# Places of matmul operands and the order of splits, taps and evacuations in a two-block layer stack

## The reference, cut to what matters

```python
# block 1
for l in range(2):
    x = x + 0.5 * swiglu(rms_norm(x, ffn1_norm[l]), ffn1_w1[l], ffn1_w2[l])      # 1024 -> 2*2816 -> 1024
    x = x + hybrid_mixer(rms_norm(x, mix_norm[l]), ...)
    x = x + 0.5 * swiglu(rms_norm(x, ffn2_norm[l]), ffn2_w1[l], ffn2_w2[l])
x = rms_norm(x, final_norm)
# its mixer: proj = h @ w_in + b_in, cut into pa, pb, pc, pg
y_a = (rg_lru(conv4(pa[:512])) * gelu(pa[512:])) @ lru_w_out      # recurrent branch
y_b = mla_branch(pb)                                              # 8 heads, low-rank q and kv
y_c = silu(layer_norm(conv31(glu(pc)))) @ conv_w_out + b          # depthwise convolution, 31 taps, 512 channels
merged = sum(sigmoid(pg)[i] * y_i); return merged @ w_out
# block 2
for l in range(2):
    x = x + rms_norm_2(hybrid_mixer_2(rms_norm_2(x)), ...)   # 4 fox, 8 nsa (selected, window, compressed), 4 dilated heads
    x = x + rms_norm_2(conv_ffn(rms_norm_2(x)), ...)         # up, 3 taps, silu(a) * b, down
```

## Time and profile before

| | |
|---|---|
| median of 3 runs | 2071.71 us (2068.88 to 2075.6) |
| profiled execution | 2077.53 us, its span 2075.7 us |
| TensorE busy, matmuls | 1994.5 us, 15240 |
| VectorE / ScalarE / GpSimd busy | 1395.0 / 1159.7 / 142.6 us |
| granted TensorE clock, mean | 0.981 |
| read from HBM | 327.27 MB, 158 GB/s over the span |
| costliest | the three products L657 to L659 with h: 2704 matmuls each, and with hid: 1056 each |

### The profile page before, as it was taken

One profiled execution on the slowest core, in us unless ns is written; L12 is line 12 of the kernel. 1 busy time (PEld: TensorE's weight loads), 2 busy tenths in 40 slices (PEclk: granted clock), 3 DMA queues, 4 the chain that ended last, 5 costly groups with the idle time before them and its releaser, 6 DMA issues.

```text
span 2075.7 us, 39521 instructions
## 1 busy us (share of the span) xinstructions
PE 1994.5 (96%) x15240; PEld 1898.6 (91%) x15240; DVE 1395.0 (67%) x2058; ACT 1159.7 (56%) x1847; POOL 142.6 (7%) x153
## 2 busy tenths in 40 slices
PE   7999989999999999999999999998999999899998
PEld 7999988999999999988999999876899998679997
DVE  5765787666655665788666656775698477638963
ACT  5444676564445444676465435665666458556753
POOL 1063100010000001100010001000200010002000
PEclk9999999999999999999999999999999999899999
DMA  5545433455545545443455544531255544203643
GB/s 210 202 166 191 168 127 132 156 189 199 171 168 199 191 154 192 170 150 109 151 193 192 184 156 168 181 123 41 102 187 181 189 144 169 102 24 140 214 156 115
DMA packets 53533, 329.80 MB, mean 159 GB/s; under 512 B 5936, under 2 KB 6704, under 8 KB 27952
## 3 DMA queue, kind: packets, MB, share of 16 engines
q1 hardware_dynamic: 53424, 328.34, 45.4%
HBM read 327.27 MB, written 1.05 MB: 158 GB/s over the span
## 4 chain that ended last, share of the span: by engine, by line
PE 66%; DVE 10%; issue 8%; ACT 5%; DVEq 4%; DMA 4%; POOLq 3%; POOL 1%; ACTq 0%; SPq 0%
PE bank L657 17%; PE bank L658 17%; PE bank L659 17%; PE bank L704 4%; DVE w_lo L636 3%; DMA raw<-in_w 3%; ACT w_hi L597 2%; PE bank L669 1%; PE bank L671 1%; DVE conv L1371 1%; PE bank L1659 1%; PE bank L1643 1%; PE bank L678 1%; DVEq L1365 1%; PE bank L1660 1%
## 5 line engine op out<-in xcount | busy, mean ns | idle before, releaser
L636 DVE TENSOR_TENSOR w_lo<-raw,w_hi 128x2048 fp32r<-128x2048 f32 (+3 forms) x348 | 673.6, 1939 | 326.5 <-ACT w_hi L597 310.6
L657 PE MATMUL bank<-h_hi,w_hi 128*128 128x256 f32 x2704 | 779.8, 288 | 12.2 <-DVE w_lo L636 4.2
L658 PE MATMUL bank<-h_lo,w_hi 128*128 128x256 f32 x2704 | 768.2, 284 | 0.0
L659 PE MATMUL bank<-h_hi,w_lo 128*128 128x256 f32 x2704 | 768.0, 284 | 0.0
L597 ACT ACTIVATE w_hi<-raw 128x2048 fp32r<-128x2048 f32 (+2 forms) x346 | 560.5, 1623 | 138.8 <-DMA raw<-in_w 117.4
L657 PEld LDWEIGHTS bank<-h_hi,w_hi 128*128 128x128 f32 x2704 | 522.2, 193 | 17.6 <-issue 11.7
L658 PEld LDWEIGHTS bank<-h_lo,w_hi 128*128 128x128 f32 x2704 | 522.1, 193 | 1.3
L659 PEld LDWEIGHTS bank<-h_hi,w_lo 128*128 128x128 f32 x2704 | 522.0, 193 | 0.0
L657 PE MATMUL bank<-hid_hi,w_hi 128*128 128x256 f32 x1056 | 295.4, 280 | 0.0
L658 PE MATMUL bank<-hid_lo,w_hi 128*128 128x256 f32 x1056 | 295.4, 280 | 0.0
L659 PE MATMUL bank<-hid_hi,w_lo 128*128 128x256 f32 x1056 | 295.4, 280 | 0.0
(11 more groups left out here) (337 smaller groups left out, 2937.3 us busy)
## 6 DMA issues: line engine op xcount, KB each, us to landing
raw<-in_w SPq DMA_DIRECT2D x198, 1024.0 KB, 4.8
raw<-in_w SPq DMA_DIRECT2D x96, 704.0 KB, 4.1
raw<-in_w SPq DMA_DIRECT2D x52, 768.0 KB, 4.2
raw<-in_w SPq DMA_DIRECT2D x8, 512.0 KB, 3.8
raw<-in_w SPq DMA_DIRECT2D x4, 576.0 KB, 3.7
x<-in_x SPq DMA_DIRECT2D x1, 1024.0 KB, 5.0
out<-x SPq DMA_DIRECT2D x4, 256.0 KB, 2.4
const<-in_const SPq DMA_DIRECT2D x1, 548.0 KB, 5.4
```

The source lines that it names most:

```text
L636: dve.tensor_tensor(w_lo[:, s % SPLIT_SLOTS, 0:n], raw[:, s % RAW_SLOTS, 0:n], w_hi[:, s % SPLIT_SLOTS, 0:n].bitcast(F32), ALU.subtract).t ...
L657: pe.matmul(out, hi, x_hi, start=start, stop=False, skip_group_check=skip)
L658: pe.matmul(out, hi, x_lo, start=False, stop=False, skip_group_check=skip)
L659: return pe.matmul(out, lo, x_hi, start=False, stop=stop, skip_group_check=skip)
```

## The change

Three things are changed.
1. Two unused tiles, of 64 bytes ahead of `x` and of 96 bytes ahead of `hid_hi`, move all that lies behind them. To stay within SBUF, `w_lat` and `rest` become smaller: `LAT_BLOCKS` is 9 instead of 10, and three blocks of uq 2 instead of two lie in `sq`. By the 32-byte rule x, h_hi and h_lo then start 64 bytes past a multiple of 128, and so do hid, m, win and o2; lat, o1 96 past; xa and conv 32 past. The weight tiles stay.
2. Block 1: pb 0 joins the steps at which VectorE (`mixer1_dve`) splits behind its taps; ScalarE's (`mixer1_act`) split behind pb 0 is dropped, so unit 9 is split with unit 10 behind li 1; the 14 taps at li 1 are 7, a split, 7; uk and uv have 1 tap each; stat_mu and stat_ln move one step later; `first_products` and `by_tiles` can take the first tiles of one unit alone (`alone`: 4 in mixer 1, 6 in the second feed-forward layer), and wait for each unit's weights on its own.
3. Block 2's mixer (`mixer2_act`, `mixer2_dve`): cum 1 moves from step 13 to 15, R 7 from 14 to 17; on ScalarE the exp of a head stands behind the transposition's copy and the W evacuation of its step; cmp 0, ca 1, cmp 1, f 6 and f 7 split nothing ahead of themselves, and units f 6, f 7, O 0 to O 3 are split behind named heads.

```diff
+LAT_BLOCKS = 9
-MU_AFTER, LN_AFTER, GATES_AHEAD = 5, 6, 2
+MU_AFTER, LN_AFTER, GATES_AHEAD = 6, 7, 2
...
-               10: [("f", 6), ("c2", 0)], 11: [("cum", 0)], 12: [("SC", 0), ("f", 7)], 13: [("cum", 1), ("R", 6)],
-               14: [("R", 7), ("TC", 0)], 16: [("J", 0)], 17: [("K", 0)], 18: [("K", 1)], 20: [("J", 1)], 21: [("K", 2)], 23: [("K", 3)],
-               25: [("K", 4)], 27: [("K", 5)]}
+               9: [("ct", 0)], 10: [("f", 6), ("c2", 0)], 11: [("cum", 0)], 12: [("SC", 0), ("f", 7)], 13: [("R", 6)],
+               14: [("TC", 0)], 15: [("cum", 1)], 16: [("J", 0)], 17: [("R", 7), ("K", 0)], 18: [("K", 1)], 20: [("J", 1)],
+               21: [("K", 2)], 23: [("K", 3)], 25: [("K", 4)], 27: [("K", 5)]}
+HIGH_BEHIND = {8: ("f", 6), 9: ("f", 7), 10: ("O", 0), 12: ("O", 2), 14: ("O", 3)}
+LOW_BEHIND = {9: ("f", 6), 10: ("f", 7), 11: ("O", 0), 12: ("O", 2), 16: ("O", 3)}
+SPLIT_BESIDE = [("cmp", 0), ("ca", 1), ("cmp", 1), ("f", 6), ("f", 7)]
...
 for n in range(3, len(HEADS2)):
-    at = EVAC2.index(("S", n))
-    EVAC2[at], EVAC2[at + 1] = EVAC2[at + 1], EVAC2[at]
+    step = EVAC2.index(("S", n))
+    EVAC2.remove(("S", n))
+    EVAC2.insert(step + (1 if n == 3 else 2), ("S", n))
...
+        sbuf("offset_h", [P, 16])
         x = sbuf("x", [P, KT, T])
...
+        sbuf("offset_hid", [P, 24])
...
-                w_lat = sbuf("w_lat", [P, 22 * P], F32, early)
+                w_lat = sbuf("w_lat", [P, (12 + LAT_BLOCKS) * P], F32, early)
...
-            sbuf("rest", [P, 3, 4, T], F32, phase)
+            sbuf("rest", [P, T + (12 + LAT_BLOCKS) * P], F32, phase)
...
-        def by_tiles(pe, work, l, groups, tile_ready, tile_used=None, stat_after=None, stat=None):
+        def by_tiles(pe, work, l, groups, tile_ready, tile_used=None, stat_after=None, stat=None, alone=0):
             outs = [(work.out(g)[:, half * T:half * T + T], s, half) for g, s in groups for half in range(2)]
-            for k in range(KT):
+            order = [(k, outs[2 * n:2 * n + 2]) for n in range(2) for k in range(alone)] + [(k, outs) for k in range(alone, KT)]
+            for k, some in order:
                 pe.wait_ge(*tile_ready(k))
+                if alone and k == 0:
+                    weights_ready(pe, some[0][1])
...
-                    first_products(pe, nm, work, l, m, [((up, j), at + j) for j in range(2)], lambda: norm_pe(pe, work, nm, l, n))
+                    if not w:
+                        weights_ready(pe, at + 1)
+                    first_products(pe, nm, work, l, m, [((up, j), at + j) for j in range(2)], lambda: norm_pe(pe, work, nm, l, n),
+                                   6 if w else 0)
...
-            weights_ready(pe, at1 + 1)
             by_tiles(pe, work, l, [(("pa", i), at1 + i) for i in range(2)], lambda k: n1.h_ready(l, KT + k + 1), n1.raw_used,
-                     3, lambda: norm_pe(pe, work, n1, l, 1))
+                     4, lambda: norm_pe(pe, work, n1, l, 1), 4)
...
-                    if i == 0:
-                        split.until(at1 + UNIT_OF[g] + AHEAD)
...
-        TAPS_AT = {("pb", 0): 6, ("pb", 1): 2, "li": 14, "pc": 4, "uq": 2, "uk": 3, "uv": 3, "S": 2, "A": 4, "B": 5}
+        TAPS_AT = {("pb", 0): 6, ("pb", 1): 2, "li": 14, "pc": 4, "uq": 2, "uk": 1, "uv": 1, "S": 2, "A": 4, "B": 5}
...
-                if g in UNIT_OF and kind not in ("A", "B", "lr", "li") and g not in LAST_OUTPUTS and g not in LAST_GATES and g != ("pc", 1):
+                if g in UNIT_OF and kind not in ("A", "B", "lr", "li") and g not in LAST_OUTPUTS and g not in LAST_GATES and g not in TAKEN_FIRST:
                     split.until(at1 + UNIT_OF[g] + AHEAD)
...
-                    convolve(TAPS_AT["li"])
+                    convolve(TAPS_AT["li"] // 2)
                     split.until(at1 + UNIT_OF[g] + AHEAD)
+                    convolve(TAPS_AT["li"] // 2)
...
                     convolve(TAPS_AT[g])
+                    if i == 0:
+                        split.until(at1 + UNIT_OF[g] + AHEAD)
...
-                if g in UNIT_OF2 and kind != "O" and g != ("vb", 1):
+                if g in UNIT_OF2 and kind != "O" and g != ("vb", 1) and g not in SPLIT_BESIDE:
                     split.until(at2 + UNIT_OF2[g] + AHEAD)
...
-                    split.until(freed_by_scores(at2, i))
+                    if i < 8:
+                        split.until(freed_by_scores(at2, i))
                     softmax_act_exp(act, probs2, row2, i % PROBS2, max2_ready(l, i + 1), exp2_ready)
                     for n in due(i, len(HEADS2)):
                         softmax_act_norm(act, probs2, row2, n % PROBS2, sums2_ready(l, n + 1), probs2_ready)
+                    if i in HIGH_BEHIND:
+                        split.until(at2 + UNIT_OF2[HIGH_BEHIND[i]])
...
-                    if i == 14:
-                        split.until(at2 + UNIT_OF2["O", 3])
+                    if i in LOW_BEHIND:
+                        split.until(at2 + UNIT_OF2[LOW_BEHIND[i]])
```

25 lines of the change are left out of this document (13 added, 12 removed), and 2 rows, old and new, of the table MIX2_BESIDE.

## The result

The changed kernel takes 2046.82 us (median of 4 runs, 2041.83 to 2047.12), the kernel before 2073.65 beside it: ratio 0.9866, interval [0.9844, 0.9889]. That is 1.3% faster, 27 us between the medians and 28 us by the ratio. The forecast was 1985 us, 4.2%. The sign is right, the size is not, and the time lies 1 us above the range. The profiled execution has a span of 2045.1 us.

The account below looks back on a forecast made before the run. TensorE's pace, set by operand place, was taken to bound the feed-forward phases. 49.4 (places) + 14.0 (mixer 1) + 23.0 (block 2's mixer) = 86.4 us off 2077.5 gives 1991.1, by the runs' median 1985; range 1936 to 2046.

Parts of the forecast that it names:

- The bound: Feed-forward phases: TensorE, busy 96%, sets the pace, 120.0 ns per matmul with h moving and 117.3 with hid, by operand place.
- Part 1: Operand places, all phases: moved tiles shorten matmul intervals; 31.0 up phases, 8.4 down phases, 10 mixers, sum 49.4 us.
- a straight line through the two places the trace has: Matmul interval by bytes past 128: 120.0 ns at 0, 117.3 at 32, so 114.7 at 64; chance 0.42, 1985 us.
- the mixers' half: Mixers: shorter matmul intervals would give 19.6 us, but another engine decides half of the time, so 10 us.
- The deep rival: All matmuls with moved operands: the extra goes entirely at 64, interval 109.5 ns, 1943 us; chance 0.28.
- The rival of 64 bytes: Operand places: only the place within 64 bytes counts, h stays at 120, hid returns to 120, 2045 us; together 0.15.
- The slower rival: Operand places: 64 is worse than 0, slower overall from an interval of 122.6 ns, 2099 us at 125; chance 0.05.
- The down phases' cap: Down phases: a raw slot's turn of 7.58 us limits each pair of units, so at most 0.24 x 48 = 11.5 us.
- Part 2: Mixer 1 and entry of the second feed-forward layer: reordered splits and taps remove TensorE waits, 2 x (1.7 + 3.3 + 2.0) = 14.0 us.
- What is late next: Mixer 1: unit 9's subtraction 0.7 us late and stat_lat behind pb 2's evacuation; of 3.5 us, 1.7 remain.
- Part 3: Block 2's mixer: two long waits and half the low clock about them go, 6.1 + 5.4 per layer, 23.0 us.
- the waits only move: Reordered mixers: each removed wait is replaced by the next link, only operand places gain, 2022 us; chance 0.10.

Follow-up runs that it names:

- Places alone: The kernel before plus the two offset tiles and the smaller spare tiles making room, no order moved: ratio 0.9933 to before, 14 us.
- the best distance with the early positions: Against the changed kernel: h, hid, m at 112 modulo 256 from weights, win, o2 at 192, position loads at start, R 7, cum 1 back: 1999.8 us.
- weights at 64: The changed kernel with the 64-byte tile ahead of w_hi instead of x, so weights, h and hid all stand at 64: ratio 0.9946 to before.
- the kernel at 192: The changed kernel with all moving operands of three-term products 192 past a multiple of 256 bytes from the weights: 2022.9 us, ratio 0.9747 to before.

## Why the forecast was wrong, point by point

- **The bound** (TensorE's pace, by operand place): right. Places alone gave 14 us with no step moved, and the best distance with the early positions gave 47 us more on nearly the same orders (only R 7 and cum 1 differ).
- **Part 1, the size.** Failed at "I take a straight line through the two places the trace has ... so 114.7 at 64". Two points were joined by a line along an axis, bytes past 128, that is not the chip's: what counts is the distance to the weights modulo 256, and it jumps (64 for hi and lo alike has 117.8 or 113.3, never 114.7). It had to be taken in full address: h stood at distance 0 of 256, hid at 160, and the change brought both to 64. At 117.8 the sum's own terms become 5856 x 2.2 = 13 us, and -3168 x 0.5 = -1.6 in the down phases, where I had +8.4. With the mixers' half, 4 us, that is 15; 14 was measured alone. A unit takes 5.65 and 3.89 us, where 5.5 and 3.79 stood forecast. This term carries 34 of the 58 us by which the sum was too large (86.4 against 28). A second fault is hidden in it: of the 31.0 us for up phases, 34 x 48 x 5.3 = 8.7 were block 2's, and block 2's up phases gave 0.1 us. Block 1's four gave 8.7. That 15 and 14 agree is therefore partly luck.
- **The deep rival** (109.5 ns, 1943 us, chance 0.28): its mechanism exists, its place and size do not: the least is 113.3. **The rival of 64 bytes** (2045 us, chance 0.15) came near the time, for the wrong reason: h did not stay at 120. **The slower rival** (64 worse than 0, from 122.6 ns) had the wrong place but a real mechanism: 123.3 ns at 4 bytes.
- **The half in the mixers.** In block 2's it seems too much: with places alone its two stretches, mixer and up phase, took 2.6 and 1.2 us longer than before, where (504 + 1056) x 2.2 ns = 3.4 us less each would follow from the intervals. The mixers had 61 us at half clock there, against 51 before. This is one execution, the slowest of its five, and not more than a hint, since the same program's mixers differ by 6 us from one execution to the next.
- **The down phases' cap.** The 7.58 us turn of a raw slot was no limit: at 113.3 ns a pair takes 66 x 113.3 = 7.48 us, and such phases take 59.84 us with no wait. Of that turn 1.85 us was waiting for a transfer; since the transfer is issued when the slot comes free, the turn can follow the pace. The forecast's "at most 0.24 x 48 pairs" does not come out of its own numbers either: from 7.74 to 7.58 are 0.16 us, 7.7 us in all, less than the 8.4 it took.
- **Part 2** (14 us): right in kind. T 0's wait (3.3), pb 1's (1.6) and the entry's (2.0) are gone. "What is late next" was named, pb 2's subtraction (0.9) and stat_lat, and the latter was costed too low: it is 2.5 us in layer 0 and 3.9 in layer 1, for q's evacuation behind two copies on ScalarE, where 1.8 us in all were taken off for both. 10 us were measured.
- **Part 3** (23 us): the step that failed is counting each long wait, and half of the low clock about it, as time gained. The waits of the earlier trace rows did go, and about the first the clock rose to 1.00. But all waits of the mixer together fell by only some 2 us in each layer (16.6 to 14.2, 16.1 to 14.4), and at the heads half clock grew from 3 to 10 us, so that block 2's mixers had 44 us of it in after against 51 before (34 to 48 in the other traces of this order). 5 us were measured. The rival "the waits only move" was the right one for this part; it should have been weighed for each part by itself, not for the whole.
- **Range and chances.** The ends were made of single cases; no case held a small gain in part 1 together with a moved part 3, and that is what came: 14 + 10 + 5 = 29 us, each measured by itself.

The Trainium skill's "TensorE: Matmul & The Clock Gate" (section "Back-to-back issue gap") gives N/2.4 + 2.5 ns, 109.2 for 256 columns, as the gap of an isolated matmul, and says itself that with a weight load for each matmul both set the spacing; the forecast left that out. No stretch reached 109.2; the runs show 113.3 to 123.3 by the places of the operands.

Open: why a distance has its interval, why some have two, and how the four tiles of a product act together. That the reads of the weights and of the moving operand hinder each other would fit that moving the weights changes it and that 256 bytes repeat it, but no run shows it. That the address of the weights enters at all rests on one kernel (weights at 64) and on stretches with w_lo moved, of which one clearly changed. Whether part 3 is worth 5 us or nothing is within the intervals.

## What to carry to other kernels

Where TensorE streams matmuls back to back, take its start-to-start interval from the timeline for each operand tile, set it against the tile's full distance to the weights, and measure a handful of distances in stretches at the end of one run before any place is chosen: here one run held 36 stretches, and the good places lie between bad ones. Measure the combination that the kernel will have, not each tile by itself. A wait that is removed inside a chain of two engines that feed each other should be counted as gained only as far as the chain itself gets shorter. Where another engine sets the pace of a stretch, a faster matmul gives nothing there: count it out for the whole of such a stretch. Before a stretch is compared between two kernels, see how much it differs between two executions of one: here 6 us in block 2's mixer. After each gain on the engine that bounds, look at engines whose work is not tied to its pace (here GpSimd, 7% busy, with its tables): they become late without having changed.

## What the hardware showed that was not expected

- The interval of 128 x 256 matmuls at full clock depends on where moving operands and weights stand to each other. With hi and lo alike it goes by the distance to the weights modulo 256 bytes: 120.0 ns at 0, 123.3 at 4, 116.7 at 16 (once 118.6) and at 32, 118.3 at 48, 117.8 or 113.3 at 64, 120.0 at 96, 113.3 at 112, 118.6 at 128, 117.3 at 160, 113.3 (in 3 of 13 stretches 117.8) at 192, 121.7 at 196. With hi and lo apart it does not follow from these: 112 with 192 gave 119.9.
- The same code at the same distance keeps one of two intervals for hundreds of matmuls. In the kernel at 192 whole phases differ by 59.84 and 62.19 us, and its runs spread from 2016.6 to 2029.2 us; at 112 from 1995.9 to 2004.0.
- One wait of 4.8 us cost 7.7: the granted clock over the 12 us about it was 0.72, and the matmuls behind it started every 0.21 us until 178.4.
